# One megabyte of the last but one expert, issued by GpSimd with its source in eight outer rows, in a one-core encoder-layer kernel

## The chip, the core and the metric

The kernel runs on one core of one Trainium2 chip. That core has five engines with instruction streams of their own: TensorE (PE in the profile), VectorE (DVE), ScalarE (ACT), GpSimd (POOL) and SyncE (SP, which issues transfers). Sixteen DMA engines move data between the chip's memory (HBM) and the on-chip buffer. The metric is the device time of one execution in microseconds. Three runs of the kernel before gave 1292.21, 1292.58 and 1292.87 us; the median is 1292.58 us.

## The reference, cut to what matters

The reference is one layer of a streaming encoder over 256 tokens of width 1024, in float32. Four mixers (a gated linear recurrence, latent attention, a complex diagonal SSM, an RG-LRU) run on one input projection and are merged, then a mixture of 32 experts follows. The change touches only how weights of this last part reach the chip:

```python
def clamped_swiglu(h):
    glu, lin = jnp.split(h, 2, axis=-1)
    glu = jnp.minimum(glu, SWIGLU_LIMIT)
    lin = jnp.clip(lin, -SWIGLU_LIMIT, SWIGLU_LIMIT)
    return glu * jax.nn.sigmoid(SWIGLU_ALPHA * glu) * (lin + 1.0)
...
    def expert_block(args):
        xb, e = args
        return clamped_swiglu(xb @ w1[e] + b1[e]) @ w2[e] + b2[e]
...
    h = layer_norm(DEEPNORM_ALPHA * x + mix, ln1_w, ln1_b)
    ffn = moe_ffn(h, router_w, router_b, moe_w1, moe_b1, moe_w2, moe_b2)
    return layer_norm(DEEPNORM_ALPHA * h + ffn, ln2_w, ln2_b)
```

Every expert has `w1` of 1024 x 2048 (8 MB) and `w2` of 1024 x 1024 (4 MB). Each token goes to its top four experts.

## The kernel before, in words

All 32 experts are computed in order, each for up to 64 tokens. The weights are far larger than the on-chip buffer, so they stream through it. An expert is six units of 2 MB, numbered 0 to 5: units 0 to 3 are `w1`, units 4 and 5 are `w2`. Ten places of 2 MB in the tensor `store` (five pairs) hold them in turn. TensorE counts each unit that it has finished with in the semaphore `expert_chunk_used`; SyncE waits on this count before it issues the transfer that overwrites the unit ten places back.

The order of the last two experts (30 and 31, `NE - 2` and `NE - 1`) is written out in the list `TAIL`: first units 0 to 3 of expert 30, then units 0 to 3 of expert 31, then units 4 and 5 of expert 30, then units 4 and 5 of expert 31. Each of the last four units is moved in two pieces of 1 MB (2048 floats on each of 128 partitions; `SLOT` is 2048) with a semaphore each (`late_landed`), so that TensorE can begin on a piece. I name a piece by expert, unit and half: 30/4/0 is the first of them, and the one that the change concerns. All these transfers are issued by SyncE on lines 454 (expert 29), 458 (the units of `w1` in `TAIL`) and 462 (the eight pieces). Two transfers of 512 KB for the last layer norm follow on lines 464 and 465.

TensorE consumes them in this order. `first_layer` multiplies the gathered tokens by units 0 to 3 of expert 31 (lines 1270 and 1278, 1278 for the fourth unit, 31/3). Then `second_half_unit` (line 1328) takes the pieces: 30/4/0, 30/4/1, 30/5/0, a transposition of the activations of expert 31 (line 1288), 30/5/1, 31/4/0, 31/4/1. Then comes half of the final combination (line 1351), the pieces 31/5/0 and 31/5/1, and the other half of the combination. VectorE and ScalarE finish with the layer norm, and the result is written out.

GpSimd makes constants at the start. Its last instruction, on line 510, clears a buffer of the recurrence early in the execution. It issues no transfer.

The line numbers of the changed kernel are one higher than these from line 462 on (the pieces stand on line 463 there), and seven higher after the new lines of GpSimd.

Of the kernel before, what the change touches and what calls it, by code (L numbers as in the profile page):

```python
# [17 lines left out]
D = 1024  # L18
# [13 lines left out]
NE = 32  # L32
# [21 lines left out]
SLOT = 2048  # L54
R1 = 8
NU = 6
NW1 = 4
UNIT = 2 * SLOT
DOUBLE = 2 * UNIT
NDBL = 5  # L60
# [41 lines left out]
def encoder_layer(nc, A, out, dbg=None):  # L102
    with ExitStack() as ctx:
        def sb(name, shape, dt=F32):
            return ctx.enter_context(nc.sbuf_tensor(name, shape, dt))

        def sem(name):
            return ctx.enter_context(nc.semaphore(name))
# [26 lines left out]
        small = sb("small", [P, 512])  # L135
# [29 lines left out]
        for i in range(2):  # L165
# [99 lines left out]
        double_landed = [sem(f"double_landed{i}") for i in range(NU)]  # L265
        late_landed = [sem(f"late_landed{i}") for i in range(8)]
        stream_total = [16 * sum(1 for i in range(1, len(STREAM)) if i % R1 == c) for c in range(R1)]
        names = """apart_landed half_used half_landed logit_read ln_used chunk_used const_ready iota_made vec_in s5_in lru_in pos_in ones_ready s5_small s5_mag s5_theta s5_trig0 c_in cT_ready f_ready trig_ready bu_psum bu_free x_ready x_used
            y_evac gelu_ready glu_psum glu_gate gate_sum yC_ready proj_evac xc_ready gate_psum gate_act soft_in soft_out sp_ready
            lru_exp lru_b2 lru_sqrt yD_ready cos_req cos_ready sq_ready ss_psum norm_ready mla_psum mla_evac mla_masked  # L270
            s_psum smax_ready sexp_ready p_norm pT_psum pT_ready o_psum o_evac lv_ready lv_psum lv_used mask_in hs_clear cross_ready
# [4 lines left out]
        S = {n: sem(n) for n in names}  # L276
# [62 lines left out]
        def unit_source(e, c):  # L339

            return double_source(e, c // 2)[:, UNIT * (c % 2):UNIT * (c % 2) + UNIT]

        def place(d):

            return (d + NDBL - 1) % NDBL * DOUBLE

        def unit_at(m):

            if m == HOME:
                return first_unit_at  # L350
            lo = place(m // 2) + UNIT * (m % 2)
            return store[:, lo:lo + UNIT]

        LAST = (NE - 1) * NU
        TAIL = [(NE - 2, c) for c in range(NW1)] + [(NE - 1, c) for c in range(NW1)]
        TAIL += [(e, c) for e in (NE - 2, NE - 1) for c in range(NW1, NU)]

        def tail_at(e, c):

            return unit_at(LAST - NU + TAIL.index((e, c)))  # L360

        def late(e, c, j):

            return 4 * (e - NE + 2) + 2 * (c - NW1) + j
        ln2_w, ln2_b = unit_at(LAST - 4)[:, 0:D], unit_at(LAST - 4)[:, D:2 * D]

        HEAD = [(0, c) for c in range(NW1)] + [(1, c) for c in range(NW1)]
# [7 lines left out]
        def _(sp):  # L375
# [79 lines left out]
            for i, (e, c) in enumerate(TAIL):  # L455
                sp.wait_ge(S["expert_chunk_used"], LAST - NU + i - 2 * NDBL + 1)
                if c < NW1:
                    sp.dma_start(tail_at(e, c), unit_source(e, c)).then_inc(unit_landed[c] if e == NE - 2 else landed[c], 16)
                else:
                    for j in range(2):  # L460
                        part = slice(SLOT * j, SLOT * j + SLOT)
                        sp.dma_start(tail_at(e, c)[:, part], unit_source(e, c)[:, part]).then_inc(late_landed[late(e, c, j)], 16)
            sp.wait_ge(S["expert_chunk_used"], LAST - 3)
# [5 lines left out]
            with sp.If(n_items > 0):  # L469
                with sp.Fori(0, n_items) as j:  # L470
                    e = sp.value_load(item_e[0:1, bass.ds(j, 1)], min_val=0, max_val=NE - 1)
# [10 lines left out]
        @block.gpsimd  # L482
        def _(pool):
            g = [0]

            def link(ins):
                g[0] += 1
                ins.then_inc(S["g_chain"], 1)
                pool.wait_ge(S["g_chain"], g[0])

            nc.gpsimd.memset(ones[:, :], 1.0).then_inc(S["ones_ready"], 1)
            link(nc.gpsimd.memset(ident[:, :], 0.0))
            link(nc.gpsimd.affine_select(out=ident[:, :], in_=ident[:, :], compare_op=ALU.not_equal, fill=1.0,
                                         base=0, pattern=[[-1, P]], channel_multiplier=1))
            nc.gpsimd.memset(ones_128[:, :], 1.0 / 128).then_inc(S["const_ready"], 1)
            nc.gpsimd.memset(ones_256[:, :], 1.0 / 256).then_inc(S["const_ready"], 1)
            nc.gpsimd.memset(half_pi[:, :], float(np.pi / 2)).then_inc(S["const_ready"], 1)
            nc.gpsimd.iota(iota_i[:, :], pattern=[[1, SEQ]], base=0, channel_multiplier=0).then_inc(S["iota_made"], 1)
            link(nc.gpsimd.memset(headmask[:, :], 1.0))
            link(nc.gpsimd.affine_select(out=headmask[:, :], in_=headmask[:, :], compare_op=ALU.is_ge, fill=0.0,  # L500
                                         base=0, pattern=[[-32, HEADS]], channel_multiplier=1))
            link(nc.gpsimd.affine_select(out=headmask[:, :], in_=headmask[:, :], compare_op=ALU.is_ge, fill=0.0,
                                         base=31, pattern=[[32, HEADS]], channel_multiplier=-1))
            link(nc.gpsimd.memset(earlier[:, :], 1.0))
            nc.gpsimd.affine_select(out=earlier[:, :], in_=earlier[:, :], compare_op=ALU.is_gt, fill=0.0,
                                    base=0, pattern=[[1, P]], channel_multiplier=-1).then_inc(S["const_ready"], 1)

            pool.wait_ge(S["x_used"], 4)
            pool.wait_ge(S["x_ready"], 8)
            nc.gpsimd.memset(hg_s, 0.0).then_inc(S["hs_clear"], 1)  # L510

        NCONST = 4

# [302 lines left out]
        def _(pe):  # L816
# [504 lines left out]
            def second_half_unit(i, c, j, turned, b):  # L1321

                pe.wait_ge(late_landed[late(NE - 2 + i, c, j)], 16)
                w = tail_at(NE - 2 + i, c).rearrange("p (k n) -> p k n", k=4)
                fh = c - NW1
                for k in (2 * j, 2 * j + 1):
                    for dh in range(2):
                        last = mm(b[64 * dh:64 * dh + 64, :], turned[:, k, 64 * fh:64 * fh + 64], w[:, k, 512 * dh:512 * dh + 512],
                                  start=(fh, k) == (0, 0), stop=(fh, k) == (1, 3))
                if j:  # L1330
                    last.then_inc(S["expert_chunk_used"], 1)
# [859 lines left out]
```

## Time and profile before

| what | value |
|---|---|
| median of three runs | 1292.58 us (1292.21 to 1292.87) |
| time of the profiled execution | 1292.49 us |
| its span, first to last instruction | 1290.6 us |
| PE busy | 1246.3 us, 97% of the span |
| PE weight loads | 645.2 us, 50% |
| DVE busy | 453.5 us, 35% |
| ACT busy | 219.0 us, 17% |
| POOL busy | 3.5 us |
| moved by DMA | 459.52 MB, mean 356 GB/s |

A busy PE need not be working at its peak. The mean over the span also mixes a first part with little data traffic (111 to 266 GB/s in most of its slices) and a second in which the DMA engines are at work nearly all of the time (about 430 GB/s). The difference between the profiled execution's time and its span is 1.89 us, which lies around the first and the last instruction.

### The profile page before, as it was taken

The page shows a single profiled execution, that of the slowest core. Times are in us where ns is not written, and L with a number is a line of the kernel's source. Part 1 is how long each engine was busy: PE and PEld are TensorE (multiplying, and loading weights), DVE is VectorE, ACT ScalarE, POOL GpSimd, SP SyncE. Part 2 cuts the span into 40 slices and gives each one's busy share as a digit, 9 for nine tenths or more (in the row PEclk, how much of TensorE's full clock was granted, in tenths as well). Part 3 has the DMA queues.
Part 4 walks back from the last instruction along what each step waited for, and adds up shares of the span by engine and source line. Part 5 has one row for each costly group of instructions (what it writes and reads, how often), then busy time and mean ns, then how long its engine had stood idle before and what let it go on. Part 6 is the DMA issues. An engine that isn't in the chain of part 4 may idle for free.

```text
span 1290.6 us, 15022 instructions
## 1 busy us (share of the span) xinstructions
PE 1246.3 (97%) x6140; PEld 645.2 (50%) x6140; DVE 453.5 (35%) x912; ACT 219.0 (17%) x429; POOL 3.5 (0%) x17
## 2 busy tenths in 40 slices
PE   9999999999999999999999899999998999999996
PEld 8888888998873333333433233333323333333331
DVE  5999924456353512122221213212121312222123
ACT  1722124231041110101101010110101010110102
POOL 0000000000000000000000000000000000000000
PEclk9999999999999999999999999999999899999999
DMA  9533344336969999999999999999999999999995
GB/s 381 199 131 140 121 143 165 117 111 237 417 266 408 428 433 431 430 432 431 432 430 431 428 435 428 433 429 433 428 433 432 429 431 431 432 428 427 429 423 220
DMA packets 30350, 459.52 MB, mean 356 GB/s; under 512 B 4656, under 2 KB 5040, under 8 KB 8400
## 3 DMA queue, kind: packets, MB, share of 16 engines
q1 hardware_dynamic: 26720, 453.00, 83.7%
q10 hardware_dynamic: 3568, 5.59, 1.3%
q8 instruction: 52, 0.85, 0.3%
q14 instruction: 10, 0.08, 0.0%
HBM read 457.53 MB, written 1.05 MB: 355 GB/s over the span
## 4 chain that ended last, share of the span: by engine, by line
PE 67%; DMA 24%; DVE 7%; ACT 1%; issue 1%; SPq 0%; DVEq 0%; POOL 0%; POOLq 0%
DMA store<-in_moe_w 24%; PE banks L1270 16%; PE banks L857 15%; PE banks L1307 12%; PE banks L871 4%; PE banks L1278 4%; PE banks L1107 2%; PE banks L1132 2%; PE banks L1366 2%; DVE store L1972 2%; PE banks L1196 1%; PE banks L1288 1%; DVE store L1969 1%; DVE store L1971 1%; DVE store L1966 1%; PE banks L845 1%
## 5 line engine op out<-in xcount | busy, mean ns | idle before, releaser
L1270 PE MATMUL banks<-store 128*64 128x512 f32 x1536 | 346.2, 600 | 18.1 <-DMA store<-in_moe_w 14.5
L1270 PEld LDWEIGHTS banks<-store 128*64 128x64 f32 x1536 | 109.5, 138 | 236.7 <-issue 211.8
L1307 PE MATMUL banks<-store 128*64 128x512 f32 x952 | 210.8, 595 | 0.0
L857 PE MATMUL banks<-store 128*128 128x256 f32 x896 | 196.7, 380 | 0.0
L857 PEld LDWEIGHTS banks<-store 128*128 128x128 f32 x896 | 169.4, 190 | 26.0 <-issue 3.4
L1966 DVE TENSOR_SCALAR store<-banks 128x512 f32<-128x512 f32 x32 | 22.1, 692 | 434.6 <-PE banks L1278 434.6
L1307 PEld LDWEIGHTS banks<-store 128*64 128x64 f32 x952 | 65.8, 137 | 142.9 <-issue 120.1
L1278 PE MATMUL banks<-store 128*64 128x512 f32 x512 | 116.8, 598 | 1.0 <-DMA store<-in_moe_w 1.0
L1980 DVE COPY store<-banks 64x512 f32<-64x512 f32 x30 | 20.8, 694 | 203.8 <-PE banks L1307 203.8
L741 ACT ACTIVATE store<-store 128x512 f32<-128x512 f32 x28 | 17.6, 630 | 435.4 <-DVE store L1966 435.4
L1278 PEld LDWEIGHTS banks<-store 128*64 128x64 f32 x512 | 34.3, 136 | 70.8 <-issue 68.1
L1196 PEld LDWEIGHTS banks<-store 128*128 128x128 f32 x480 | 56.9, 191 | 23.5 <-issue 23.5
L1196 PE MATMUL banks<-store 128*128 128x128 f32 x480 | 63.7, 281 | 0.0
L1366 PE MATMUL banks<-store 128*128 128x512 f32 x120 | 63.5, 631 | 0.0
L871 PE MATMUL banks<-store 128*128 128x256 f32 x256 | 56.3, 380 | 0.1
L871 PEld LDWEIGHTS banks<-store 128*128 128x128 f32 x256 | 48.3, 190 | 7.4 <-issue 1.0
L730 ACT ACTIVATE store<-banks,ln_cols 128x128 f32<-128x128 f32 x128 | 46.4, 475 | 3.1 <-PE banks L1196 1.9
L749 ACT ACTIVATE store<-banks 64x512 f32<-64x512 f32 x28 | 16.5, 589 | 169.5 <-PE banks L1307 169.5
L1366 PEld LDWEIGHTS banks<-store 128*128 128x128 f32 x120 | 19.1, 188 | 43.8 <-issue 43.8
L1990 DVE TENSOR_TENSOR store<-store,banks 128x512 f32<-128x512 f32 x60 | 37.4, 682 | 0.9 <-PE banks L1385 0.8
L1132 PE MATMUL banks<-store 32*64 32x512 f32 x256 | 34.8, 613 | 0.0
L1972 DVE SCALAR_TENSOR_TENSOR store<-store 128x512 f32<-128x512 f32 x32 | 33.6, 1050 | 1.1
(375 smaller groups left out, 844.9 us busy)
## 6 DMA issues: line engine op xcount, KB each, us to landing
store<-in_moe_w SPq DMA_DIRECT2D x72, 4096.0 KB, 35.2
store<-in_moe_w SPq DMA_DIRECT2D x39, 2048.0 KB, 15.6
store<-in_w_in SPq DMA_DIRECT2D x30, 1024.0 KB, 5.0
store<-in_moe_w SPq DMA_DIRECT2D x17, 1024.0 KB, 21.8
store<-in_w_branch SPq DMA_DIRECT2D x8, 1024.0 KB, 4.8
store<-in_w_out SPq DMA_DIRECT2D x4, 1024.0 KB, 6.0
store<-in_w_first SPq DMA_DIRECT2D x2, 512.0 KB, 5.8
store<-in_xT ACTq DMA_DIRECT2D x2, 512.0 KB, 6.2
```

Source lines behind the costliest of these rows:

```text
L730: ins = nc.scalar.activation(xg[:, k, :], src, ACT.Identity, scale=ln1_cols[:, 2 * KD + k:2 * KD + k + 1], bias=ln1_cols[:, 3 * KD + k:3 * ...
L857: last = mm(b[:, j * SEQ:(j + 1) * SEQ], w[:, k, j * P:j * P + P], xT[:, k, :], start=k == 0, stop=k == KD - 1)
L871: last = mm(bank[3 + u % 2][:, i * SEQ:(i + 1) * SEQ], w[:, k, c * P:(c + 1) * P], yT[:, br, k, :], start=k == 0, stop=k == 3)
L1132: mm(bank[into[i]][64 * ct:64 * ct + 64, :], esel[r:r + NE, :], b1_all[r:r + NE, :], start=True, stop=False, tile_position=(r, 64 * ct))
L1196: last = mm(bank[2 + k // 4][:, (k % 4) * P:(k % 4) * P + cols], h_tok[:, half, k * P:k * P + P], sel[:, half, 0:cols], start=half == 0, s ...
L1270: last = mm(bank[into[i]][64 * ct:64 * ct + 64, :], xg[:, 2 * c + kk, col:col + CAP], w[:, kk, i * FF + ct * 512:i * FF + ct * 512 + 512], ...
L1278: last = mm(bank[into[i]][64 * ct:64 * ct + 64, :], xg[:, 2 * c + kk, col:col + CAP], w[:, kk, i * FF + ct * 512:i * FF + ct * 512 + 512], ...
L1307: last = mm(bank[4][64 * dh:64 * dh + 64, :], actT[:, j, 64 * fh:64 * fh + 64], w[j][:, 512 * dh:512 * dh + 512], start=(fh, j) == (0, 0), ...
L1366: mm(bank[COMB_BANK[i]][:, :], wselT[0:rows_, half, :], y_pair[0:rows_, 512 * dh:512 * dh + 512], start=True, stop=True).then_inc(S["comb_ ...
L1966: V.tensor_scalar(g1, bank[from_[0]][:, :], LIMIT, None, ALU.min).then_inc(S["gmin_ready"], 1)
L1972: V.scalar_tensor_tensor(g1.rearrange("p (j q) -> p q j", j=4), g2.rearrange("p (q j) -> p q j", j=4), 1.0, g3.rearrange("p (q j) -> p q j ...
L1990: ins = V.tensor_tensor(dst, dst, bank[COMB_BANK[i]][:, :], ALU.add)
```

## The change

The piece 30/4/0 is no longer issued by SyncE. GpSimd issues it instead, after the same count of `expert_chunk_used` that SyncE waits for ahead of the second piece of that unit. Its source is a new input, `w2_rows`, which holds the same 1 MB in another order, and is read with dimensions 8 x 16 x 2048; the destination is the same 128 partitions x 2048 floats. Ahead of it GpSimd issues a transfer of 8 rows of 16 floats (512 bytes) from the same input into a free corner of the tensor `small`, and waits until it has landed. `late_landed` of the piece gets the same 16 as before.

```diff
+        APART_ROWS = (NE - 2, NW1)
...
-                    for j in range(2):
+                    for j in range((e, c) == APART_ROWS, 2):
                         part = slice(SLOT * j, SLOT * j + SLOT)
                         sp.dma_start(tail_at(e, c)[:, part], unit_source(e, c)[:, part]).then_inc(late_landed[late(e, c, j)], 16)
...
             nc.gpsimd.memset(hg_s, 0.0).then_inc(S["hs_clear"], 1)
+
+            e, c = APART_ROWS
+            pool.wait_ge(S["expert_chunk_used"], LAST - NU + TAIL.index((e, c)) - 2 * NDBL + 1)
+            pool.dma_start(small[0:8, 320:336], A["w2_rows"][0, :, 0:16]).then_inc(S["first_rows"], 16)
+            pool.wait_ge(S["first_rows"], 16)
+            pool.dma_start(tail_at(e, c)[:, 0:SLOT], A["w2_rows"].rearrange("b a n -> a b n")).then_inc(late_landed[late(e, c, 0)], 16)
...
+    arrays["in_w2_rows"] = _np.ascontiguousarray(arrays["in_moe_w2"][NE - 2, :, 0:2 * D].reshape(8, 16, 2 * D).transpose(1, 0, 2))
```

On SyncE, at the end of the weight stream (`in_moe_w1` and `in_moe_w2` are the experts' weights, `128x4096` floats a whole unit and `128x2048` a piece), these rows stand before:

```order
L458 DMA store<-in_moe_w1 128x4096 [waits expert_chunk_used] x8
L462 DMA store<-in_moe_w2 128x2048 [waits expert_chunk_used]
L462 DMA store<-in_moe_w2 128x2048
L462 DMA store<-in_moe_w2 128x2048 [waits expert_chunk_used]
L462 DMA store<-in_moe_w2 128x2048
```

and these now:

```order
L459 DMA store<-in_moe_w1 128x4096 [waits expert_chunk_used] x8
L463 DMA store<-in_moe_w2 128x2048 [waits expert_chunk_used] x2
L463 DMA store<-in_moe_w2 128x2048
L463 DMA store<-in_moe_w2 128x2048 [waits expert_chunk_used]
L463 DMA store<-in_moe_w2 128x2048
```

One row of 128x2048, the one directly behind the units of `w1`, is gone; the waits of the others are the same.

On GpSimd, behind its constants, the end of the program is now this (before, it ended with the row of the MEMSET into `store` and the branch):

```order
L505 MEMSET earlier 128x128 [waits g_chain]
L506 AFFINE_SELECT earlier<-earlier 128x128 [waits g_chain]
L511 MEMSET store 128x1024 [waits x_ready,x_used]
L515 DMA small<-in_w2_rows 8x16 [waits expert_chunk_used]
L517 DMA store<-in_w2_rows 128x1x2048 [waits first_rows]
L103 UNCONDITIONAL_BRANCH
```

The two transfers are the last things that GpSimd does. No other engine's program moves.

## Rows read from the trace of the kernel before

**Rows 1.** The chain that ended last, shares of the whole span.
```profile
PE 67%; DMA 24%; DVE 7%; ACT 1%; issue 1%; SPq 0%; DVEq 0%; POOL 0%; POOLq 0%
```
**Rows 2.** The same chain from 1219 us on: start us, us, what.
```profile
1184.16 41.78 DMA store<-in_moe_w
...
1229.75 4.11 SPq L462
...
1233.90 36.37 DMA store<-in_moe_w
1270.27 0.04 issue
1270.31 1.94 PE banks L1328 x8
```
**Rows 3.** Timeline, engine PE: start us, us, line, xcount [idle before <-releaser].
```profile
1243.37 3.65 PE L1270 MATMUL banks<-store 128*64 128x512 f32 x16
1246.95 0.66 PE L1339 MATMUL banks<-ident,store 128*128 128x128 f32 x4
...
1255.49 3.65 PE L1278 MATMUL banks<-store 128*64 128x512 f32 x16 [0.87 <-DMA store<-in_moe_w]
1258.95 3.63 PE L1328 MATMUL banks<-store 128*64 128x512 f32 x16
1262.87 1.94 PE L1328 MATMUL banks<-store 128*64 128x512 f32 x8 [0.28 <-DMA store<-in_moe_w]
1264.73 0.66 PE L1288 MATMUL banks<-ident,store 128*128 128x128 f32 x4
1265.35 1.94 PE L1328 MATMUL banks<-store 128*64 128x512 f32 x8
1267.92 1.94 PE L1328 MATMUL banks<-store 128*64 128x512 f32 x8 [0.63 <-DMA store<-in_moe_w]
1270.31 1.94 PE L1328 MATMUL banks<-store 128*64 128x512 f32 x8 [0.45 <-DMA store<-in_moe_w]
1272.17 1.99 PE L1351 MATMUL banks<-store 64*128 64x512 f32 x8
1274.09 3.65 PE L1328 MATMUL banks<-store 128*64 128x512 f32 x16
```
**Rows 4.** Stretches: A:B us, PE, PEld, DVE, ACT, POOL busy, PEclk, DMA share, GB/s.
```profile
1100.00:1200.00 100.00, 94.91 (x444) 33.65 (x444) 20.64 (x45) 12.60 (x28) 0.00 (x0) 1.00 1.00 428
1268.00:1269.00 1.00, 1.00 (x6) 0.47 (x8) 0.03 (x1) 0.00 (x0) 0.00 (x0) 1.00 0.99 406
1269.00:1270.00 1.00, 0.86 (x5) 0.00 (x0) 0.00 (x0) 0.00 (x0) 0.00 (x0) 1.00 0.75 307
1270.00:1275.00 5.00, 4.69 (x20) 1.51 (x22) 0.00 (x0) 0.00 (x0) 0.00 (x0) 1.00 0.52 218
1276.00:1277.00 1.00, 1.00 (x8) 0.29 (x5) 0.00 (x0) 0.00 (x0) 0.00 (x0) 1.00 0.10 41
```
**Rows 5.** DMA queues of the whole span: packets, MB, share of 16 engines.
```profile
q8 instruction: 52, 0.85, 0.3%
```
**Rows 6.** Line 462: duration ns min/median/max, first and last start us, time to landing.
```profile
L462 SPq DMA_DIRECT2D store<-in_moe_w x8: 340/3532/4252, 1219.0 to 1242.5; - x8
...
DMA to landing us min/median/max: 32.7/38.5/40.9
```
**Rows 7.** DMA issues: xcount, KB each, median us to landing.
```profile
store<-in_moe_b ACTq DMA_DIRECT2D x4, 64.0 KB, 12.6
ln_cols<-in_ln_cols ACTq DMA_DIRECT2D x1, 16.0 KB, 2.8
```
**Rows 8.** Timeline, engines ACT and DVE, around the transposition on line 1288.
```profile
1260.38 1.08 DVE L1972 SCALAR_TENSOR_TENSOR store<-store 128x512 f32<-128x512 f32 x1
1265.43 0.60 ACT L759 ACTIVATE store<-banks 128x512 f32<-128x512 f32 x1 [6.61 <-PE banks L1288]
1277.79 0.69 DVE L2070 COPY store<-banks 64x512 f32<-64x512 f32 x1 [9.76 <-PE banks L1328]
```

More of the change, by code:

```diff
@@ L267, in encoder_layer @@
         stream_total = [16 * sum(1 for i in range(1, len(STREAM)) if i % R1 == c) for c in range(R1)]
-        names = """apart_landed half_used half_landed logit_read ln_used chunk_used const_ready iota_made vec_in s5_in lru_in pos_in ones_ready s5_small s5_mag s5_theta s5_trig0 c_in cT_ready f_ready trig_ready bu_psum bu_free x_ready x_used
+        names = """apart_landed first_rows half_used half_landed logit_read ln_used chunk_used const_ready iota_made vec_in s5_in lru_in pos_in ones_ready s5_small s5_mag s5_theta s5_trig0 c_in cT_ready f_ready trig_ready bu_psum bu_free x_ready x_used
             y_evac gelu_ready glu_psum glu_gate gate_sum yC_ready proj_evac xc_ready gate_psum gate_act soft_in soft_out sp_ready
```

## The prediction, made before the changed kernel ran

> **What bounds the kernel now.** I read the page's chain first. TensorE holds 67% of it and transfers 24% [rows 1], so the question is which of the two holds the end, where the change lies. The chain from 1219 us on answers it [rows 2]: long pieces of DMA, the last of them until 1270.27 us, and TensorE starts on line 1328 at 1270.31. That is piece 31/4/1. From there to the end everything is computation: the pieces of expert 31's unit 5 are there when TensorE comes to them.
>
> Next the timeline of TensorE [rows 3]. Its waits for data at the end are four: 0.87 us ahead of line 1278 (unit 31/3), then 0.28, 0.63 and 0.45 ahead of pieces 30/5/0, 31/4/0 and 31/4/1. The first matters for this change, since it stands in the stream ahead of the piece that is moved. The other three stand behind it.
>
> Third, the stretches [rows 4]. In 1100 to 1200 us the DMA share is 1.00 at 428 GB/s, so all sixteen DMA engines work without a pause. At the end this doesn't stop at once. The share is 0.99 until 1269 us, 0.75 in the next, and then 0.52 for five microseconds at 218 GB/s, and some work is left until past 1276 us. Every transfer of the stream spans 128 partitions, so all engines have the same to do; half of them (eight) have finished about 7 us (1269.5 to some 1276.3) ahead of the other half. I call them the front half and the rear half. Two things follow. A transfer counts as landed when its last share is there, so TensorE always waits for the rear half. And the rear half isn't faster when the front half is done (218 GB/s is 0.51 of 428), so the limit is in each engine, and bytes taken from the rear half save its time in full.
>
> Why there is a rear half, the page suggests [rows 5]: instruction loads take 0.3% of sixteen engines' span, 0.003 x 16 x 1290.6 = 62 us of engine time. If eight engines carry all of it, that is 7.7 us each, close to the 7 us of lead.
>
> **The change part by part.** The sum is made against the profiled execution, 1292.49 us (span 1290.6 and 1.89 around it), 0.09 us under the median of 1292.58.
>
> 1 MB is 1,048,576 bytes; at 428 GB/s over sixteen engines [rows 4] it costs each engine 2.45 us. Over eight engines, at 214 GB/s, it costs each of these 4.90 us. The source of the moved piece has an outer dimension of eight, which I read as a deal into eight shares. So eight engines get 4.90 - 2.45 = 2.45 us more work than before, the other eight 2.45 us less. The Trainium skill says this in its page "DMA: Bandwidth & Descriptors", section "Why a DMA increments its semaphore by 16 and not by 1": the number of engines is the largest up to 16 that divides the slowest dimensions of both sides, here 8, and for GpSimd they are consecutive ones from a cursor that goes round. No run here has shown it yet. By it the 512 bytes, 8 rows, take the first eight engines, and the piece the other eight.
>
> Removed on SyncE: one issue of line 462, 0.34 to 4.25 us of its time [rows 6]. The pieces are issued 33 to 41 us ahead of their landing, so I cost it at nothing: the queue hides it. With that cover gone it would be worth at most 4.25 us.
>
> Added on GpSimd: a wait and two transfers. Nothing is queued behind them, and only piece 30/4/0 waits for them. The wait ends where SyncE's does, at 1219.0 us [rows 6]. What 512 bytes on a GpSimd queue take, no row shows. The nearest rows are small transfers of another queue, 2.8 us in a quiet stretch and 12.6 us beside the stream [rows 7]; I take 2.8 to 12.6, and the piece goes out between 1222 and 1232 us. Sharing its eight engines with SyncE's queue it takes 4.90 us at the least, 10 if they alternate evenly, 15 if SyncE's 16 KB rows go against its 8 KB rows. It lands between 1227 and 1247 us and is needed at 1258.95 [rows 3]: at least 12 us to spare.
>
> The piece is now carried out earlier than its place in SyncE's queue, so what is ahead of that place (units 31/0 to 31/3 among it) comes up to 4.90 us later on the eight engines that carry it. Put on the front half, this costs nothing: a lead of 7 us shrinks to 2.1, and the rear half still lands last, when it did before. So unit 31/3 and line 1278 stay at 1255.49. If the lead of the slowest engine of the front half were less than 4.90, the difference would be lost there; the DMA share of 0.75 at 1269 to 1270 [rows 4] says that some leave later than others.
>
> Behind the moved piece the rear half is 2.45 us ahead of before, the front half 2.45 us behind. The lead becomes 7 - 4.9 = 2.1 us, still a lead, so the landings of 30/4/1 to 31/5/1 move by the full -2.45 us. What TensorE can use of it is less, since its waits are short. Sixteen matmuls of such a unit take 3.58 us until the next can start (1243.37 to 1246.95), eight take 1.86 (1262.87 to 1264.73) [rows 3]:
> - 30/5/0 could start at 1258.95 + 3.58 = 1262.53 and started at 1262.87: 0.34 us.
> - 31/4/0 could start at 1265.35 + 1.86 = 1267.21, started at 1267.92: 0.71 us.
> - 31/4/1 could start at 1267.92 + 1.86 = 1269.78, started at 1270.31: 0.53 us.
>
> Sum 1.58 us. None is limited by the landings afterwards: 31/4/1 lands at 1270.27 - 2.45 = 1267.82 and starts at 1270.31 - 1.58 = 1268.73; the others have more room. Nor by the helpers: the transposition on line 1288 needs line 1972, done at 1261.46, and would now start at 1264.39; 31/4/0 needs the copy on line 759, which ends at 1266.03 - 0.34 = 1265.69 and is needed at 1266.87 [rows 8]. What is late next is TensorE itself from 1255.49 to 1278 us, and then VectorE's copy on line 2070, which moves with it. The 0.87 us ahead of line 1278 stay.
>
> What GpSimd's first transfers cost around the span (their set-up, a longer end) no row shows. The difference between time and span is 1.89 us now; I take nothing, and would not be surprised by 0.5 us. Together: 1292.49 - 1.58 = 1290.9 in the profiled execution, 1291.0 as the median.
>
> **The rivals.**
>
> *The rear half carries it.* No row tells which eight engines are in front; this is the weak point. Then units 31/0 to 31/3 land up to 4.90 us later, and line 1278 starts at 1260.39 instead of 1255.49. From there TensorE has no waits left, which gives 1.58 back: +3.3 us, 1295.9. The landings behind allow it (31/4/1 at 1270.27 + 2.45 = 1272.72, TensorE there at 1273.6). It decides as soon as one of the eight engines belongs to the rear half, since the last share counts. For it: a blind choice of eight would hit it half of the time or more. Against it: the lighter half is one block of eight by its count, the 512 bytes move the deal by one block, and I hold it likelier, with no row for it, that the instruction loads begin with the block of the first engine.
>
> *All sixteen carry it.* Then nobody is relieved, and the piece only overtakes: line 1278 starts 2.45 us later, 1.58 comes back, +0.9 us, 1293.4. For it speaks that a destination of 128 partitions is dealt to sixteen everywhere in this trace. The same page of the Trainium skill, section "Issuing engines are not separate DMA queues", says that who issues doesn't matter, since all queues share the same sixteen engines; by that rule alone moving the issue gains nothing, and this is its price here.
>
> *The time is kept elsewhere.* The front half is slowed by its own share more than the 4.90 us (a second queue on an engine costs switching, GpSimd's transfers cost a start), and line 1278 starts 1 to 2 us later, which eats the gain: about 1292.6. For it: the slowest engine of the front half may lead by little more than 5 us. Against: nothing in the trace shows such losses.
>
> *The piece comes late.* It decides when the piece lands after 1258.95, 40 us after GpSimd's wait ends. That is as long as SyncE's own queue takes [rows 6], so it needs that GpSimd's queue is served behind SyncE's; with 12.6 us for the first and 40.9 us for the second transfer it would be 1272.5 and 13 us lost, 1306.
>
> **How the numbers follow.** Forecast, front half with eight engines: 0.58. Rear or mixed: 0.20. All sixteen: 0.09. Kept elsewhere: 0.10. Late: 0.03. The likeliest gives 1291.0, its own range 1290.3 to 1292.0: the lower end, if some of the 0.87 us ahead of line 1278 goes too, the upper one, if half of the sum is lost to small costs. The range for 8 in 10 reaches to the rear-half case: 1290.3 to 1296.1. A measurement of this kernel can tell about 0.2%, 2.6 us. The sum is below this, so it counts as no change even where it comes. Faster by over 0.2% needs more than all four waits (1.58 + 0.87 = 2.45): 0.06. Slower by over 0.2% (above 1295.2): most of the rear half and the late case: 0.20. Within: 0.74.
>
> **What would show it.** In the changed profile: a GpSimd queue with a little over 1 MB; line 1278 at the same time as before against the rows ahead of it, with its wait of about 0.9 us; the three waits of line 1328 gone; a DMA share that falls from 1.00 later and reaches zero about 2.4 us sooner, the stretch at half share some 2 us long instead of 7. Wrong would be: that stretch grown to 12 us and line 1278 waiting 5 us (rear half), the stretch as long as before (all sixteen), or line 1328's first start waiting for GpSimd's transfer (late).

## The result, and the profile after

The changed kernel took 1304.56 us (median of four runs, 1303.49 to 1305.58), the kernel before on the same chip 1292.72 us. The ratio is 1.0091, with a 95% interval of 1.0079 to 1.0103: about 12 us slower, where I had forecast 1291.0 and a range up to 1296.1. The profiled execution took 1305.58 us, with a span of 1303.6.

The timeline of TensorE in the changed kernel shows where the time goes. The columns are those of [rows 3]; lines 1277, 1285, 1335 and 1358 are the former 1270, 1278, 1328 and 1351.

```profile
1235.36 1.13 PE L1373 MATMUL banks<-store 128*128 128x512 f32 x2
1244.70 5.56 PE L1285 MATMUL banks<-store 128*64 128x512 f32 x16 [8.21 <-DMA store<-in_moe_w]
...
1254.77 3.65 PE L1277 MATMUL banks<-store 128*64 128x512 f32 x16 [0.66 <-DMA store<-in_moe_w]
...
1259.58 3.65 PE L1277 MATMUL banks<-store 128*64 128x512 f32 x16 [0.57 <-DMA store<-in_moe_w]
1265.35 5.35 PE L1277 MATMUL banks<-store 128*64 128x512 f32 x16 [2.12 <-DMA store<-in_moe_w]
1270.50 3.63 PE L1285 MATMUL banks<-store 128*64 128x512 f32 x16
1273.93 5.35 PE L1335 MATMUL banks<-store 128*64 128x512 f32 x24
1279.21 0.66 PE L1295 MATMUL banks<-ident,store 128*128 128x128 f32 x4
1279.80 5.37 PE L1335 MATMUL banks<-store 128*64 128x512 f32 x24
1285.10 1.99 PE L1358 MATMUL banks<-store 64*128 64x512 f32 x8
```

The row that answers to the first long wait, unit 30/3 in the kernel before, is this:

```profile
1235.77 3.65 PE L1278 MATMUL banks<-store 128*64 128x512 f32 x16 [0.17 <-DMA store<-in_moe_w]
```

The reader is to see three things. Unit 30/3, which stands far ahead of the moved piece in the stream, begins 8.93 us later (1235.77 to 1244.70), behind a wait of 8.21 us. Unit 31/3 begins 15.01 us later (1255.49 in [rows 3], 1270.50 here). And the waits ahead of the pieces on line 1335 are gone, as forecast: twenty-four matmuls and then twenty-four more run without a wait, and half of the combination on line 1358 begins 12.93 us later, so 2.1 us came back on the way. The loss is made before the pieces are reached, not at them.

The stretches show what the transfers did. The columns are those of [rows 4].

```profile
1225.00:1230.00 5.00, 5.00 (x25) 1.53 (x21) 0.00 (x0) 0.00 (x0) 0.62 (x1) 1.00 1.01 419
1230.00:1235.00 5.00, 4.26 (x18) 1.26 (x18) 0.00 (x0) 0.00 (x0) 0.00 (x0) 1.00 1.03 257
...
1240.00:1245.00 5.00, 0.30 (x2) 0.30 (x4) 0.00 (x0) 0.00 (x0) 0.00 (x0) 0.50 1.01 254
1245.00:1250.00 5.00, 5.00 (x16) 1.23 (x12) 0.81 (x2) 0.63 (x1) 0.00 (x0) 0.64 1.02 256
...
1255.00:1260.00 5.00, 4.43 (x22) 1.65 (x20) 1.63 (x8) 0.66 (x2) 0.00 (x0) 1.00 1.00 423
```

From 1229 to 1252 us the sixteen DMA engines are as busy as before (share 1.0), but they move 247 to 257 GB/s instead of 428. Busy here means that packets are under way, and each takes longer: the 128 packets of 8 KB that make up the moved piece took 0.50 us each (the median in the trace), and those of the same piece in the run pool16 below 0.31 us. A reader who looks at the share alone misses it; the rate beside it tells. One row over the stretch gives the sum:

```profile
1229.00:1252.00 23.00, 14.04 (x46) 3.95 (x42) 2.74 (x4) 0.63 (x1) 0.00 (x0) 0.78 1.02 263
```

23 us at 263 GB/s do the work of 23 x 263 / 428 = 14.1 us: 8.9 us of the stream are lost. GpSimd's issues on the timeline and the time that its piece took, from line 517's view, say what ran in that stretch:

```profile
1219.99 0.66 POOL L515 DMA_DIRECT2D small<-in_w_rows  x1 [1034.71 <-PE banks L1314]
1225.79 0.62 POOL L517 DMA_DIRECT2D store<-in_w_rows  x1 [5.14 <-DMA small<-in_w_rows]
```
```profile
DMA to landing us min/median/max: 28.1/28.1/28.1
```

The piece is issued at 1225.8 us and lands at 1253.9; its packets run from 1229.6 to 1252.4 us. The slow stretch is the time in which it is carried.

What the lateness is made of is read at unit 31/2, the last for which TensorE waits. In the kernel before, TensorE took up units 30/3 and 31/3 as they landed, at 1235.77 and 1255.49 us, four units apart, so one unit lands every 4.93 us and 31/2 was there at about 1250.6. Here 31/2 is taken up as it lands at 1265.35 us: 14.8 us later. The low rate accounts for 8.9 us of this. Another 4.90 us is what an engine pays that carries an eighth of the piece ahead of these units, as a unit counts as landed only with its last share, and the last shares here fit engines that carried the piece (the table further down has what speaks for it; the trace names no engines). Together 13.8 us; the last 1.0 us is open.

TensorE's clock adds next to nothing. After the long wait its granted clock is down to 0.50 (1.2 GHz; 0.50 in 1240 to 1245 us), and the sixteen matmuls of unit 30/3 take 5.56 us instead of 3.65; those of unit 31/2 take 5.35 us. But behind 30/3 TensorE waits for data again, 0.66, 0.57 and 2.12 us, so the first delay is taken up by these waits. The second can only be the step from 14.8 us at 31/2 to 15.0 us at 31/3. Less the 2.1 us that come back at the pieces, that is the 12.9 us.

### The profile page after: what moved, and what is told of

It reads as the page before. It is cut to its first block, busy times and chain, and to the rows that moved or that the text cites. A ratio compares the mean times of both kernels' runs of the same rounds, so it can differ in the third digit from the quotient of the medians.

```text
span 1303.6 us, 15023 instructions
## 1 busy us (share of the span) xinstructions
PE 1248.1 (96%) x6140; PEld 647.2 (50%) x6140; DVE 453.5 (35%) x912; ACT 219.2 (17%) x429; POOL 4.7 (0%) x19
## 4 chain that ended last, share of the span: by engine, by line
PE 69%; DMA 21%; DVE 7%; ACT 1%; issue 1%; another core or an unknown queue 0%; DVEq 0%; SPq 0%; POOL 0%; POOLq 0%
DMA store<-in_moe_w 21%; PE banks L1277 16%; PE banks L864 15%; PE banks L1314 12%; PE banks L1285 4%; PE banks L878 4%; PE banks L1114 2%; PE banks L1139 2%; DVE store L1979 2%; PE banks L1373 2%; PE banks L1203 1%; PE banks L1295 1%; DVE store L1976 1%; DVE store L1978 1%; DVE store L1973 1%; PE banks L1335 1%
```

## The experiments

All are variants of the changed kernel. Shown is what differs from it, and times are medians beside the kernel before on the same chip. The two questions were what makes the stream slow, and what this says of the forecast. Theory A laid it to the deal of the transfer into eight shares, theory B to a second queue fed by GpSimd, theory C to the order of the rows in memory.

**pool16: GpSimd issues the piece in the ordinary deal.**

```diff
-            pool.dma_start(tail_at(e, c)[:, 0:SLOT], A["w2_rows"].rearrange("b a n -> a b n")).then_inc(...)
+            pool.dma_start(tail_at(e, c)[:, 0:SLOT], unit_source(e, c)[:, 0:SLOT]).then_inc(...)
```

> GpSimd still issues the small transfer and then the piece, but the piece's source is the ordinary one (128 rows of 8 KB), so that nothing asks for a deal into eight. Theory A (the deal into eight shares slows all sixteen DMA engines while it is under way): no slow stretch, GB/s stays near 428 in 1230 to 1250 us, the time 1293 to 1294 us (the overtaking alone: +0.9). Theory B (a second queue that GpSimd feeds slows the engines, however the piece is dealt): a stretch at about 255 GB/s again, 1302 to 1306 us.

Measured: 1293.55 us, ratio 1.0001 (0.9991 to 1.0010). The stretch in which the piece is carried, and TensorE's one wait for data from unit 30/2 on:

```profile
1230.00:1237.00 7.00, 6.31 (x24) 1.65 (x20) 0.00 (x0) 0.00 (x0) 0.00 (x0) 1.00 1.00 421
```
```profile
1238.37 5.33 PE L1285 MATMUL banks<-store 128*64 128x512 f32 x16 [2.06 <-DMA store<-in_moe_w]
...
1262.16 5.32 PE L1335 MATMUL banks<-store 128*64 128x512 f32 x24
...
1268.00 5.37 PE L1335 MATMUL banks<-store 128*64 128x512 f32 x24
```

421 GB/s with GpSimd's queue beside SyncE's: theory B falls. This is also the prediction's case of all sixteen engines (+0.9 us) in the flesh: the overtaking shows as a wait of 2.06 us, earlier than I had put it (at unit 30/3, not 31/3), and the waits at the pieces are gone in return.

**act8: ScalarE issues the eight-share transfer.** GpSimd issues nothing.

```diff
             expert(NE - 3, 1, NPAIR - 2, NPAIR - 1)
+            act.dma_start(tail_at(*APART_ROWS)[:, 0:SLOT], A["w2_rows"].rearrange("b a n -> a b n")).then_inc(...)
```

> ScalarE issues the piece (new input, outer dimension of eight) on its own queue behind its last work on expert 29, within 1 to 4 us of where GpSimd did; no small transfer ahead. Theory A: the rate falls to about 255 GB/s for some 20 us, 1302 to 1306 us. Theory B: rate near 428, 1290 to 1297 us according to which eight engines carry it.

Measured: 1303.52 us, ratio 1.0083 (1.0066 to 1.0100). The stretch:

```profile
1227.00:1249.00 22.00, 13.36 (x38) 3.65 (x36) 0.00 (x0) 0.00 (x0) 0.00 (x0) 0.79 1.00 257
```

The same loss with another issuer. It is the deal or the memory order.

**sp8: SyncE issues it in the old place.**

```diff
-                    for j in range((e, c) == APART_ROWS, 2):
+                    for j in range(2):
                         part = slice(SLOT * j, SLOT * j + SLOT)
+                        from_ = A["w2_rows"].rearrange("b a n -> a b n") if (e, c, j) == (*APART_ROWS, 0) else unit_source(e, c)[:, part]
```

> SyncE issues the piece in its old place in the stream, from the new input with its outer dimension of eight; GpSimd issues nothing. Theory A: while this piece is under way the rate falls to about 255 GB/s or, with eight engines taking it alone, somewhat less; nothing runs beside it on the same engines, so the loss is shorter: 1294 to 1302 us. Theory B: no loss of rate beyond the uneven deal, 1290 to 1296 us. The order of the rows in memory as the cause (theory C) expects the same loss as theory A here.

Measured: 1304.00 us, ratio 1.0079 (1.0062 to 1.0095), above the range that I gave for theory A: I had thought that without a second queue the loss would be shorter. It isn't:

```profile
1247.00:1269.00 22.00, 14.98 (x58) 4.66 (x52) 2.93 (x4) 1.29 (x3) 0.00 (x0) 0.84 1.01 258
```

The piece lies in SyncE's own queue here, and what stands behind it in the same queue goes on beside it on the other engines, just as slowly.

**pool8_no_start: the changed kernel without the 512 bytes.**

```diff
-            pool.dma_start(small[0:8, 320:336], A["w2_rows"][0, :, 0:16]).then_inc(S["first_rows"], 16)
-            pool.wait_ge(S["first_rows"], 16)
```

> The changed kernel without the 512-byte transfer and the wait for it. If the small transfer moves the deal to another eight engines, the other eight carry the piece now. Theory A and B alike: the same slow stretch of about 20 us, some 5 us earlier, with another outcome of which engines are last: 1298 to 1310 us. If the slow stretch comes only from the block that the small transfer leads to, it is gone: 1290 to 1297 us.

Measured: 1304.17 us, ratio 1.0081 (1.0064 to 1.0098); 22 us at 256 GB/s, from 1225 us on, 4 us earlier than in the changed kernel. The small transfer, and with it the block of eight engines that it may lead to (the trace doesn't name engines), makes no difference to the loss.

**sp8_in_order: the memory order of the partitions.** As sp8, with the rows of a block one behind the other in memory and a gap of 4 KB between blocks, so that the source still has an outer dimension of eight.

```diff
-    arrays["in_w2_rows"] = ...reshape(8, 16, 2 * D).transpose(1, 0, 2))
+    rows_ = _np.zeros((8, 16 * 2 * D + 1024), _np.float32)
+    rows_[:, 0:16 * 2 * D] = arrays["in_moe_w2"][NE - 2, :, 0:2 * D].reshape(8, 16 * 2 * D)
```

> As sp8, but the eight blocks of sixteen rows lie in memory in the order of the partitions (each engine reads 128 KB in one run, with a gap of 4 KB behind it), so only the memory order differs from sp8. Theory C (the order of the rows in memory slows the reads): the slow stretch is gone, 1293 to 1296 us. Theory A1 and A2: as sp8, 1302 to 1306 us.

Measured: 1303.26 us, ratio 1.0076 (1.0059 to 1.0093); 24 us at 241 GB/s. Theory C falls.

**sp16_rows: sixteen shares of eight neighbouring rows.** As sp8, but the host reshapes to (16, 8, 2D) before the transposition.

> As sp8 (SyncE issues the piece in its old place), but the source has an outer dimension of sixteen with eight rows each, so that all sixteen engines carry it and each would write eight neighbouring partitions. Theory A1 (it is the partitions that a share writes: several engines write to one group of partitions at a time, and they hold up the rest): still a slow stretch, shorter than in sp8, 1295 to 1301 us. Theory A2 (it is the use of only eight engines): none, 1292 to 1294 us.

Measured: 1298.59 us, ratio 1.0043 (1.0027 to 1.0060). The stretch:

```profile
1246.00:1262.00 16.00, 12.88 (x54) 4.43 (x52) 0.69 (x1) 0.66 (x2) 0.00 (x0) 0.89 1.00 274
```

A slow stretch again, without the number eight. So it isn't the use of only half of the engines (A2), if the sixteen rows are dealt to all sixteen, as I take it. What is left is which partitions an engine writes (A1), or the two-level shape of the source by itself, which this run doesn't separate.

**sp8_four and act8_four: eight shares of four rows.** The megabyte goes as four transfers of 32 partitions, by SyncE in the old place or by ScalarE beside the stream, and TensorE waits for all four (64 on the semaphore).

```diff
+            for r in range(4):
+                act.dma_start(tail_at(*APART_ROWS)[32 * r:32 * r + 32, 0:SLOT], A["w2_rows"][r].rearrange("b a n -> a b n")).then_inc(...)
...
-    arrays["in_w2_rows"] = ...reshape(8, 16, 2 * D).transpose(1, 0, 2))
+    arrays["in_w2_rows"] = ...reshape(4, 8, 4, 2 * D).transpose(0, 2, 1, 3))
```

> SyncE issues the piece in its old place as four transfers of 32 partitions, each with an outer dimension of eight and four rows, so that eight engines carry the megabyte, but each of them writes a group of four partitions of its own at a time. TensorE waits for all four. Theory A1: no slow stretch, rate near 428, and the time shows the uneven deal alone: 1290.5 to 1291.5 us if the eight engines are the front half, 1293 to 1296 us if they are the rear half. Theory A2: a slow stretch as in sp8, 1300 to 1306 us.

> As sp8_four, but ScalarE issues the four transfers on its own queue where it did in act8, so that the piece overtakes SyncE's queue. Theory A1: no slow stretch; 1291.0 us if the eight engines are the front half, 1295.9 us if they are the rear half (the two cases of the prediction). Theory A2: about 255 GB/s for 20 us, 1302 to 1306 us.

Measured: 1300.80 us, ratio 1.0058 (1.0042 to 1.0075), and 1297.98 us, ratio 1.0036 (1.0023 to 1.0048). Theory A1 missed both. Theory A2 has the first in its range (1300 to 1306) and missed the second (1302 to 1306), though sp16_rows speaks against its reason. The stretches of act8_four show why. The first row is the time of the first two transfers (partitions 0 to 63), the second that of the last two (64 to 127):

```profile
1226.00:1234.00 8.00, 6.04 (x26) 1.92 (x24) 0.00 (x0) 0.00 (x0) 0.00 (x0) 0.97 1.01 428
1234.00:1246.00 12.00, 8.76 (x31) 2.50 (x28) 1.21 (x2) 0.63 (x1) 0.00 (x0) 0.88 1.01 298
```

Full rate for the first half, 298 GB/s for the second, with the same issuer, shape and number of shares. (In sp8_four the two halves can't be told apart, since SyncE's queue reaches the front and the rear engines some 6 us apart; its stretch from 1250 to 1266 us ran at 265 GB/s.) I formed theory O from this: the loss comes when an engine writes partitions that another engine serves in the ordinary deal. If ScalarE's eight shares go to the lowest eight engines, partitions 0 to 63 in groups of four are their own, 64 to 127 are foreign. The page "DMA: Bandwidth & Descriptors" of the Trainium skill gives such a map in its section "The descriptor swizzle": for 128 partitions, engine = 8 x (partition >> 6) + ((partition >> 2) & 7), and each engine writes one port of the buffer. It doesn't say what leaving the map costs; the two rows above do.

**pool8_own and pool8_foreign: the map, put to the test.** The same four transfers by GpSimd, whose eight-share transfers would fall in turn on the lower and the upper eight engines. In the one order every engine gets its own partitions, in the other those of the other half.

```diff
-            pool.dma_start(small[0:8, 320:336], ...)
-            pool.wait_ge(S["first_rows"], 16)
-            pool.dma_start(tail_at(e, c)[:, 0:SLOT], A["w2_rows"].rearrange("b a n -> a b n")).then_inc(...)
+            for r in (0, 2, 1, 3):      # pool8_foreign: (2, 0, 3, 1)
+                pool.dma_start(tail_at(e, c)[32 * r:32 * r + 32, 0:SLOT], A["w2_rows"][r].rearrange("b a n -> a b n")).then_inc(...)
```

> GpSimd issues the piece as four transfers of 32 partitions with an outer dimension of eight, in the order 0-31, 64-95, 32-63, 96-127, with no small transfer ahead. If eight-share transfers of GpSimd fall in turn on the lower and the upper eight engines, each engine writes only partitions that it writes in an ordinary transfer. Theory O (the loss comes when an engine writes partitions that another engine serves in the ordinary deal, as in the second half of act8_four): no slow stretch, 1293 to 1295 us, like pool16. Theory E (the number of engines, or the shape of the source): about 255 GB/s for 15 to 25 us, 1301 to 1306 us.

> The same four transfers in the order 64-95, 0-31, 96-127, 32-63, so that every engine writes partitions of the other half, one group of four each. Theory O: a slow stretch for the whole piece, 255 to 285 GB/s for 15 to 25 us, 1299 to 1305 us. Theory E: no difference to pool8_own. If both orders are alike and half slow, the turn of the engines is not as assumed.

Measured: pool8_own 1292.94 us, ratio 1.0001 (0.9991 to 1.0010); pool8_foreign 1299.84 us, ratio 1.0055 (1.0038 to 1.0071). The stretches, first of pool8_own:

```profile
1222.00:1237.00 15.00, 13.35 (x59) 4.16 (x55) 0.69 (x1) 0.59 (x1) 0.68 (x2) 1.00 1.00 420
```

then of pool8_foreign:

```profile
1224.00:1243.00 19.00, 13.35 (x47) 3.87 (x44) 0.00 (x0) 0.00 (x0) 0.00 (x0) 0.82 1.02 287
```

The order of four numbers alone makes the difference of 420 and 287 GB/s and of 7 us. Theory O holds, and theory E (the number of engines or the shape of the source) falls. O and the turn of the engines are tested together here: one order is at full rate throughout and the other slow throughout, as they give it with the first transfer on the lower eight and the next on the upper eight. The trace names no engines, so it can't show the turn by itself; the cursor that the Trainium skill describes, in the section that the prediction names, agrees with it.

**pool8_half: half of the bytes.** The eight-share transfer takes only 1024 of the 2048 columns; SyncE issues the rest in the ordinary deal, and TensorE waits for both.

```diff
+            pool.dma_start(tail_at(e, c)[:, 0:D], A["w2_rows"].rearrange("b a n -> a b n")[:, :, 0:D]).then_inc(S["first_rows"], 16)
```

> The changed kernel with only the first 1024 of the 2048 columns in the eight-share transfer (512 KB) and no small transfer ahead; SyncE issues the other 512 KB in the ordinary deal at the piece's old place. If the loss grows with the bytes written in the foreign deal: the slow stretch is 10 to 13 us instead of 23, and the time 1297 to 1299.5 us. If it is a fixed price of such a transfer: 1302 to 1306 us.

Measured: 1296.72 us, ratio 1.0030 (1.0020 to 1.0040), a little under the range. The stretch:

```profile
1224.00:1239.00 15.00, 9.78 (x38) 3.03 (x36) 0.00 (x0) 0.00 (x0) 0.00 (x0) 0.84 1.02 312
```

15 us at 312 GB/s lose 15 x (1 - 312 / 428) = 4.1 us of the stream, against 8.9 for the whole megabyte. I had expected 10 to 13 us; the stretch is longer and less slow, but its loss is about half. The price goes with the bytes and isn't fixed.

No variant beat the kernel before. The two that don't lose, pool16 and pool8_own, are level with it within 0.1%.

## Why the prediction was wrong, point by point

**The step that failed** is the sentence "Sharing its eight engines with SyncE's queue it takes 4.90 us at the least, 10 if they alternate evenly, 15 if SyncE's 16 KB rows go against its 8 KB rows", and the reading under it, that "the limit is in each engine, and bytes taken from the rear half save its time in full". I read 218 GB/s at half share [rows 4] as proof that engines don't share a limit, and carried it over to a deal that the trace had never seen. It holds as long as each engine writes its own partitions. In the new deal each share is, as I read it, sixteen neighbouring partitions, most of which other engines serve; the piece took about 23 us to carry instead of at most 15, and all sixteen engines slowed down with it, to 0.61 of the rate (263 / 428). This term was missing from the sum. It cost 8.9 us of the stream.

A second step failed beside it: "Put on the front half, this costs nothing". Unit 31/3 didn't stay where it was. The units ahead were held up on the engines that land last, and that is worth another 4.90 us (the table below).

**The rivals.** The rear half or a mixed eight, which I gave 0.20, came true in its own term: "It decides as soon as one of the eight engines belongs to the rear half, since the last share counts". Its 1295.9 us lacks the 8.9 us of the low rate; with them it is 1304.8. For these the nearest rival was that the time is kept elsewhere, "the front half is slowed by its own share more than the 4.90 us". Right in kind, but I let it take 1 to 2 us and wrote "nothing in the trace shows such losses". The trace could show none, as all its transfers are dealt alike; that is a missing bound, not a bound of nothing. The cost of the unseen operation should have been open upward, and the range with it.

**The overtaking** (2.45 us later for the units ahead with sixteen carriers, 4.90 with eight) was right in mechanism and size. pool16 shows it alone, as a wait of 2.06 us. Its place was wrong: I looked for it at unit 31/3, but the units that it meets first are those whose landing TensorE is just waiting for, 30/3 above all (its wait was 0.17 us before, so it had no slack). I had left unit 30/3 out of the account.

**The 1.58 us of the three waits** came back, and 0.5 us more: in the changed kernel, in pool16 and in pool8_own no piece is waited for. From the first start of line 1328 to the combination the kernel before took 13.22 us (1258.95 to 1272.17, [rows 3]), the changed one 11.17 (1273.93 to 1285.10). I had taken 1.86 us for eight matmuls; in a row without waits twenty-four take 5.28 (1273.93 to 1279.21), 1.76 for eight. The term was outweighed by ones that I didn't have.

**All sixteen engines**: forecast +0.9 us; pool16 measured 1293.55 us beside 1293.16, a ratio of 1.0001, too close to tell from nothing or from 0.9.

**Late arrival**: GpSimd's 512 bytes took 5.5 us, inside my 2.8 to 12.6. The piece landed at 1253.9 us, later than my 1227 to 1247, but still 5 us ahead of the 1258.95 at which the kernel before needs it. Not the cause.

**Front half and rear half.** The last stretches of the changed kernel, 1 us each, show something that neither case had:

```profile
1279.00:1280.00 1.00, 1.00 (x8) 0.62 (x8) 0.00 (x0) 0.09 (x1) 0.00 (x0) 1.00 0.86 360
1283.00:1284.00 1.00, 1.00 (x8) 0.29 (x5) 0.00 (x0) 0.00 (x0) 0.00 (x0) 1.00 0.20 82
1285.00:1286.00 1.00, 1.00 (x6) 0.49 (x6) 0.00 (x0) 0.00 (x0) 0.00 (x0) 1.00 0.14 57
1288.00:1289.00 1.00, 1.00 (x8) 0.36 (x6) 0.00 (x0) 0.00 (x0) 0.00 (x0) 1.00 0.11 45
```

The share is 0.86 (fourteen of sixteen at work), then 0.14 to 0.11 (two). So the extra bytes did bring most of the front half level with most of the rear half, but two engines were the last by some 5 us. At the pieces this cost nothing, as TensorE was later still. At the units ahead of them it did cost: of the sixteen shares of unit 31/3 the trace has fourteen landed by 1264.2 us, 8.8 us after the last one in the kernel before (1255.4), and the other two at 1269.4 and 1270.2. The runs bear out that these two are late because they carried an eighth of the piece. The start of unit 31/3 later than the 1255.49 us of the kernel before should be the loss of the stream, worked out from each run's slow stretch as above, and 4.90 us where eight engines carry the megabyte, 2.45 where sixteen do (or eight carry half of it):

| run | loss of the stream, us | overtaking, us | sum | start of 31/3 later by, us |
|---|---|---|---|---|
| changed kernel | 8.9 | 4.90 | 13.8 | 15.0 |
| pool8_no_start | 8.8 | 4.90 | 13.7 | 14.2 |
| act8 | 8.8 | 4.90 | 13.7 | 13.1 |
| act8_four | 3.6 | 4.90 | 8.5 | 8.3 |
| pool8_half | 4.1 | 2.45 | 6.5 | 6.8 |
| pool8_foreign | 6.3 | 2.45 | 8.7 | 8.9 |
| pool8_own | 0.3 | 2.45 | 2.7 | 3.1 |
| pool16 | 0.1 | 2.45 | 2.6 | 3.2 |

The starts in the last column are those of the rows of unit 31/3, here of act8_four and of pool8_foreign:

```profile
1263.79 3.65 PE L1282 MATMUL banks<-store 128*64 128x512 f32 x16 [1.28 <-DMA store<-in_moe_w]
```
```profile
1264.38 3.65 PE L1284 MATMUL banks<-store 128*64 128x512 f32 x16 [0.83 <-DMA store<-in_moe_w]
```

The sums hold within 1.2 us in all eight; with 2.45 in every row the four that have 4.90 would fall short by 1.9 to 3.7 us. Which engines the late ones are stays open: that the block held six engines in front and two behind would explain two late ones in the changed kernel, but the traces of pool8_no_start, act8 and act8_four have two late shares of 31/3 as well, though their eight need not be the same. That the leading engines lead because the instruction loads [rows 5] go to the others was not tested either.

Could the idea work at all? With theory O, hardly, as an argument and not from a run: the front half may only write its own partitions at full rate, and each partition needs the same number of bytes. What pool8_own does (own partitions, half of the engines per transfer) is the ordinary deal again.

## What to carry to other kernels

Bytes can't be moved freely between DMA engines: a load whose outer dimension isn't the plain run of 128 partitions may send engines to partitions that others serve, and then the core's other transfers slow down with it, the ones already queued too. And a transfer that overtakes the queue delays what is ahead of it by the time of its most loaded engine, not by the mean over all of them (4.90 us here, not 2.45). When the DMA share stays at 1.00, read the GB/s beside it; a transfer that slows the rest shows there and nowhere else. And where a change brings a form of transfer that the trace doesn't hold, its price has no upper bound from the rows: try it first in the ordinary form (pool16 here), then in the new one.

## What the runs showed of the hardware that I had not expected

- With one 1 MB transfer in the eight-share deal under way, the core's rate is 257 GB/s (act8), 258 (sp8), 256 (pool8_no_start), instead of 428, whoever issues it and in whichever queue it lies. With sixteen shares of eight rows it is 274 (sp16_rows), with one foreign group of four partitions per engine 287 to 298 (pool8_foreign, act8_four), with own groups 420 to 428.
- GpSimd's queue costs nothing visible in itself: 421 GB/s beside SyncE's stream, and 11.5 us from issue to landing for 1 MB in the ordinary deal (pool16), against 28.1 us in the eight-share deal.
- What the resource is that the foreign writes hold up is open. That it is the way into the buffer and not the read side follows only from sp8_in_order and the two orders of pool8_own and pool8_foreign, whose reads are alike.
- A wait of TensorE of 8.21 us was followed by matmuls at half clock: 5.56 us for sixteen, where 3.65 is usual. Waits of 2.06 us (pool16) and 2.12 us (the changed kernel) were followed by the same, 5.33 and 5.35 us; that of 0.87 us [rows 3] was not. The length of the wait alone doesn't decide: behind 3.24 us (act8_four) and 3.65 us (sp8_in_order) sixteen matmuls took the usual 3.65.
